# Modulation blocks in the two-stream norms, and four edits beside them, in a float32 network on one core

## The chip, the cores and the metric

The kernel runs on one core of a Trainium2 chip. The metric is the device time of one execution in microseconds (us), lower is better. TensorE is called PE here, VectorE DVE, ScalarE ACT, GpSimd POOL, SyncE SP.

## The reference

The reference is two networks one after the other, all in float32. The first has two layers on two streams, `x` (256 tokens) and `ctx` (256 tokens), width 1024. Each layer computes 9 modulation vectors per stream from `c` and `c_ctx`, and then runs feed-forward, token mixing, feed-forward, each between a norm before and a norm after:

```python
for l in range(DEPTH):                                   # 2
    mx = mod_vectors(c, w_mod[l], b_mod[l])              # silu(c) @ w_mod + b_mod, in 9 parts
    mc = mod_vectors(c_ctx, w_mod[l], b_mod[l])
    x   = sandwich_ffn(x,   gate_up[l, 0], down[l, 0], g[0], g[1], mx[0], mx[1], mx[2])
    ctx = sandwich_ffn(ctx, gate_up[l, 0], down[l, 0], g[0], g[1], mc[0], mc[1], mc[2])
    hx, hc = modulate(rms_norm(x, g[2]), mx[3], mx[4]), modulate(rms_norm(ctx, g[2]), mc[3], mc[4])
    out_x, out_c = token_mix(hx, hc, w_in[l], w_out[l], ...)
    x = x + mx[5] * rms_norm(out_x, g[3])                # ctx the same, but not in the last layer
    x = sandwich_ffn(x, gate_up[l, 1], down[l, 1], g[4], g[5], mx[6], mx[7], mx[8])
```

Token mixing turns queries and keys by rotary factors (cos and sin times the element and its partner 16 rows away), runs attention, and a pooling branch. The second network has four blocks on `x` alone, each with a mixer, a layer norm, an MLP, a layer norm, and a gated projection.

## The kernel before

Every engine walks the same Python program (`walk`) and keeps only its own instructions, so each engine's order is the program order written there. Activations stand as [128 partitions, 8 tiles of channels, tokens]; two-stream stages have n = TT = 512 tokens, one-stream stages n = T = 256.

**Product stages.** Weights come in slots of 1 MB (`w_raw`, four slots, DMA issued by SP, L407). `cut` makes a high part on ACT (`w_hi`, L422) and a low part on DVE (`w_lo`, L425). `slot_products` runs three matmuls per tile pair (L433 to L435): 16 x 3 matmuls for one full slot.

**Modulation.** `w_mod` has 36 blocks of 256 columns per layer, 72 in all. `mod_rows` handles one block: POOL loads two halves of 512 KB into `m_raw` (two buffers, L494), each load waiting until PE has used the same buffer's last content; PE multiplies each half by the two condition vectors (L505), four column groups side by side. After four blocks DVE copies the rows (L512) and `mod_turn` turns them into vectors (L527, L533). The first 8 blocks come from early loads (`m_first`, issued by SP) between the first norm's sums and its tiles. The other 64 are put into product stages, one ahead of a weight slot (`mod_per` in `gemm` and `gate_up`): in layer 0's first feed-forward 16 in gate/up, 8 in the first down product and 4 in the second; in its second feed-forward 16, 8 and 6; in layer 1's first feed-forward 6.

**Norms.** After a product stage `post_norm` waits with `border()` for all engines, takes the root of the sums (`inverse_root`: ACT square root L852, DVE reciprocal L856), and PE broadcasts the result to all partitions with four 128x128 matmuls (`spread`, L781). DVE scales and adds, tile by tile (L944, L949). `pre_norm` of the next stage follows in `pre_sums`: per channel tile k an ACT square (L794) and a PE sum (L774), in lockstep with DVE's tiles by two `tmp_g` buffers; then `inverse_root` again, and DVE and ACT make `a_hi` and `a_lo` (L913, L918, L925), for which the first slot's products wait tile by tile. There are four two-stream pairs of post and pre norm (after both layers' first feed-forward, after layer 0's mixing and second feed-forward).

**repeat_bias.** In both first feed-forwards, just ahead of `post_norm`, POOL issues seven DMAs (L1107) that rewrite a bias table from DRAM to DRAM. POOL reaches them after its last `m_raw` load of the second down product.

**Rotary.** `rope_na` runs between the products of the pooling input: 8 matmuls against a permutation (`na_swap`, L1226), and 24 small DVE operations.

**Layer norms of the second network.** `product_norm` gathers its sums during the products; `centre_of_first` (L1495) sits between the first and second half of pair 1, group 0. Its chain at the end has two broadcasts, `far` and `root`.

Of the kernel before, what the change touches and what calls it, by code (L numbers as in the profile page):

```python
# [29 lines left out]
P = 128  # L30
# [47 lines left out]
class Place:  # L78


    def __init__(self):
        self.slot, self.side, self.tables, self.mod_layer, self.mod_slot = 0, 0, 0, 0, 0
        self.a_ready = None
        self.a_order = None
        self.x_ready = None
# [70 lines left out]
def constants():  # L156
# [5 lines left out]
    swap = np.zeros((P, P), np.float32)  # L162
    for p in range(P):
# [6 lines left out]
        swap[p + (ROPE_PAIRS if first else -ROPE_PAIRS), p] = 1.0  # L170
    c["na_cos"], c["na_sin"], c["na_swap"] = cos, sin, swap
# [44 lines left out]
def build(nc, A, out, upto=99):  # L216

    with ExitStack() as ctx:
# [42 lines left out]
        with ExitStack() as h:  # L261
# [8 lines left out]
            Z["na_swap"] = sb("na_swap_s", [P, P], F32, h)  # L270
# [79 lines left out]
        def walk(who, e):  # L350
# [58 lines left out]
            def cut(m, i=None, step=0, halves=(0, 1)):  # L409
# [3 lines left out]
                for half in halves:  # L413
                    c = slice(half * P, half * P + P)
                    raw, hi, lo = w_raw[:, m % RAW, :, c], cut_slot(w_hi, m)[:, :, c], cut_slot(w_lo, m)[:, :, c]
                    if act:
# [5 lines left out]
                        e.activation(hi, raw, ACT.Copy).then_inc(S.hi_ready.sem, 1)  # L422
                    if dve:
                        e.wait_ge(S.hi_ready.sem, val(2 * m + half + 1, i, 2 * step))
                        e.tensor_tensor(lo, raw, hi.bitcast(F32), ALU.subtract).then_inc(S.lo_ready.sem, 1)  # L425
# [56 lines left out]
            def mod_rows(i, j, per):  # L482


                layer, ms = at.mod_layer, at.mod_slot + j
                w = matrix(A["w_mod"][layer])
# [3 lines left out]
                for half in range(2):  # L490
                    k0 = 4 * half
                    if pool and own >= 1:
                        e.wait_ge(S.mod_used.sem, val(2 * count + half - 1, i, 2 * per))
                        e.dma_start(m_raw[:, half, :, :], w[:, k0:k0 + 4, ms * SC:ms * SC + SC] if i is None  # L494
                                    else w[:, k0:k0 + 4, bass.ds(e.snap(i * (per * SC) + ms * SC), SC)]).then_inc(mod_landed[half], 16)
                    if pe:
                        if half == 0 and r == 0 and batch > 0:
                            e.wait_ge(S.mod_rows.sem, val(batch, i, batches))
                        if own >= 1:
                            e.wait_ge(mod_landed[half], val(16 * own, i, 16 * per))  # L500
                        elif half == 0:
                            e.wait_ge(first_landed[count], 32)
# [43 lines left out]
            def mods(passes, per):  # L546

                def body(i, first):
                    for j in range(per):
                        mod_rows(i, j, per)  # L550
                        if j:
                            mod_turn(i, j - 1, per)
# [1937 lines left out]
```

## Time and profile before

| | us |
|---|---|
| runs (3) | median 3280.05, 3278.34 to 3292.75 |
| profiled execution, own time | 3276.89 |
| its span | 3274.9 |
| PE busy | 3064.8 (94%) |
| DVE busy | 1678.6 (51%) |
| ACT busy | 1354.5 (41%) |
| POOL busy | 213.9 (7%) |

The busy share of PE counts pipelined matmuls as busy and averages over stages. The norms show as stretches in which the granted PE clock falls and PE is idle; the page's slices hide them, the windows show them.

### The profile page before, as it was taken

Reading aid. Unit: us, or ns where it says so; the run is one execution under the profiler, and the core shown is the slowest. Engines: PE = TensorE matmul, PEld = TensorE weight load, DVE = VectorE, ACT = ScalarE, POOL = GpSimd, SP = SyncE. Lnnn points to the kernel's source line nnn. Section 1 sums busy time; section 2 is a strip of 40 time slices with the busy share of each in tenths; the row PEclk is TensorE's granted clock in tenths of the full one; section 3 lists DMA queues with packets and bytes.
Section 4 is the critical chain, followed back from the end, with each engine's and each line's share of the span. In section 5 each row is a group of like instructions: output and inputs, shape, how many; then the busy total and the mean of one; then the engine's idle time right before and its main releaser. Section 6 shows DMA issues by size and latency. Waiting matters only on the chain. (4 is left out here: it accounts for less than half of the span.)

```text
span 3274.9 us, 52918 instructions
## 1 busy us (share of the span) xinstructions
PE 3064.8 (94%) x21712; PEld 2694.9 (82%) x21712; DVE 1678.6 (51%) x2574; ACT 1354.5 (41%) x2092; POOL 213.9 (7%) x304
## 2 busy tenths in 40 slices
PE   6999989989999899997989899998999999988998
PEld 4777858657777688876789889998799989988998
DVE  3332254552322633235655557656675677556765
ACT  3222232632222432223455455546464555454644
POOL 1111014101110000011200000000000000000000
PEclk9999989989999899998989999999899999989999
DMA  8555344135554223253245543554265546543553
GB/s 275 167 179 171 99 133 124 40 104 179 177 167 145 90 90 102 91 163 117 67 146 191 167 154 112 185 168 137 65 193 193 160 146 202 191 141 104 168 193 104
DMA packets 405772, 474.85 MB, mean 145 GB/s; under 512 B 10860, under 2 KB 383164, under 8 KB 405578
## 3 DMA queue, kind: packets, MB, share of 16 engines
q1 hardware_dynamic: 380176, 389.05, 36.9%
q0 software_dynamic: 24544, 82.74, 8.0%
q8 instruction: 144, 2.36, 0.3%
q10 hardware_dynamic: 858, 0.29, 0.0%
q14 instruction: 50, 0.41, 0.0%
HBM read 470.84 MB, written 4.84 MB: 145 GB/s over the span
## 5 line engine op out<-in xcount | busy, mean ns | idle before, releaser
L425 DVE TENSOR_TENSOR w_lo<-w_raw,w_hi 128x1024 fp32r<-128x1024 f32 x734 | 897.3, 1228 | 1268.8 <-ACT w_hi L422 1267.7
L433 PE MATMUL bank<-a_hi,w_hi 128*128 128x256 f32 (+1 forms) x3864 | 1241.3, 321 | 57.8 <-DVE a_lo L1398 16.6
L434 PE MATMUL bank<-a_lo,w_hi 128*128 128x256 f32 (+1 forms) x3864 | 1227.1, 318 | 0.0
L435 PE MATMUL bank<-a_hi,w_lo 128*128 128x256 f32 (+1 forms) x3864 | 1226.3, 317 | 0.0
L422 ACT ACTIVATE w_hi<-w_raw 128x1024 fp32r<-128x1024 f32 x734 | 771.1, 1056 | 987.5 <-PE bank L435 957.1
L433 PEld LDWEIGHTS bank<-a_hi,w_hi 128*128 128x128 f32 x3864 | 741.2, 192 | 134.5 <-issue 76.0
L435 PEld LDWEIGHTS bank<-a_hi,w_lo 128*128 128x128 f32 x3864 | 741.5, 192 | 50.5
L434 PEld LDWEIGHTS bank<-a_lo,w_hi 128*128 128x128 f32 x3864 | 741.4, 192 | 47.7
L433 PE MATMUL bank<-h_hi,w_hi 128*128 128x256 f32 (+1 forms) x1728 | 544.5, 315 | 0.0
L435 PE MATMUL bank<-h_hi,w_lo 128*128 128x256 f32 (+1 forms) x1728 | 539.6, 312 | 0.0
L434 PE MATMUL bank<-h_lo,w_hi 128*128 128x256 f32 (+1 forms) x1728 | 539.5, 312 | 0.0
L433 PEld LDWEIGHTS bank<-h_hi,w_hi 128*128 128x128 f32 x1728 | 325.8, 189 | 29.9 <-issue 7.4
L435 PEld LDWEIGHTS bank<-h_hi,w_lo 128*128 128x128 f32 x1728 | 324.7, 188 | 21.1
L434 PEld LDWEIGHTS bank<-h_lo,w_hi 128*128 128x128 f32 x1728 | 325.0, 188 | 20.0
L494 POOL DMA_DIRECT2D m_raw<-in_w_mod x128 | 95.6, 751 | 1162.7 <-PE bank L505 1017.3
L636 ACT ACTIVATE h_hi<-tmp_y 128x256 f32 (+3 forms) x216 | 94.7, 477 | 84.9 <-DVE tmp_y L689 83.8
L640 DVE TENSOR_TENSOR h_lo<-tmp_y,h_hi 128x256 f32 (+3 forms) x216 | 99.7, 502 | 11.3 <-ACT h_hi L636 9.5
L1682 ACT ACTIVATE tmp_g<-bank 128x256 f32<-128x256 f32 x128 | 49.1, 383 | 128.4 <-PE bank L435 128.4
L774 PE MATMUL bank<-tmp_g,ones 128*32 128x64 f32 (+1 forms) x1040 | 52.8, 292 | 49.7 <-ACT tmp_g L794 46.9
L433 PE MATMUL bank<-w_hi,a_hi 128*128 128x256 f32 (+1 forms) x288 | 82.9, 288 | 10.7 <-DVE v_g L763 10.7
L710 ACT ACTIVATE z<-bank 128x512 f32<-128x512 f32 (+1 forms) x48 | 25.2, 526 | 156.2 <-PE bank L435 156.1
L1107 POOL DMA_DIRECT2D xt<-in_p x4 | 2.9, 732 | 1295.2 <-DVE a_lo L1398 676.9
(289 smaller groups left out, 2320.7 us busy)
## 6 DMA issues: line engine op xcount, KB each, us to landing
w_raw<-in_mlp_w SPq DMA_DIRECT2D x128, 1024.0 KB, 5.3
w_raw<-in_w_ffn_gate_up SPq DMA_DIRECT2D x88, 1024.0 KB, 5.3
m_raw<-in_w_mod POOLq DMA_DIRECT2D x128, 512.0 KB, 4.8
w_raw<-in_w_ffn_down SPq DMA_DIRECT2D x32, 1024.0 KB, 5.9
w_raw<-in_gla_w_in SPq DMA_DIRECT2D x24, 1024.0 KB, 5.5
w_raw<-in_w_in SPq DMA_DIRECT2D x16, 1024.0 KB, 6.0
w_raw<-in_ple_w_gate SPq DMA_DIRECT2D x16, 1024.0 KB, 5.1
w_raw<-in_w_ffn_down SPq DMA_DIRECT2D x16, 768.0 KB, 6.2
```

The source lines that it names most:

```text
L422: e.activation(hi, raw, ACT.Copy).then_inc(S.hi_ready.sem, 1)
L425: e.tensor_tensor(lo, raw, hi.bitcast(F32), ALU.subtract).then_inc(S.lo_ready.sem, 1)
L433: e.matmul(dst, hi, rhs_hi, start=start, stop=False)
L434: e.matmul(dst, hi, rhs_lo, start=False, stop=False)
L435: return e.matmul(dst, lo, rhs_hi, start=False, stop=stop)
L494: e.dma_start(m_raw[:, half, :, :], w[:, k0:k0 + 4, ms * SC:ms * SC + SC] if i is None else w[:, k0:k0 + 4, bass.ds(e.snap(i * (per * SC) ...
L636: e.activation(hidden_at(h_hi_f, p, m, i, per, n), tmp_y[:, m, 0:n], ACT.Copy).then_inc(S.hidden_hi.sem, 1)
L640: e.tensor_tensor(hidden_at(h_lo_f, p, m, i, per, n), tmp_y[:, m, 0:n], hidden_at(h_hi_f, p, m, i, per, n).bitcast(F32), ALU.subtract).the ...
L710: e.activation(dst, b[m][:, 0:n], ACT.Copy).then_inc(S.act_evicted.sem, 1)
L774: mm = e.matmul(dst[32 * g:32 * g + 32, 0:w], ones[:, 0:32], src[:, g * w:g * w + w], start=start, stop=stop)
L1107: e.dma_start(dst, src).then_inc(side_sem, 16)
L1682: e.activation(tmp_g[:, m, 0:T], b[m][:, 0:T], ACT.Relu).then_inc(S.act_evicted.sem, 1)
```

## The change

1. `mod_rows` is split into `mod_load` (POOL), `mod_half` (PE, one half block) and `mod_copy` (DVE). A generator, `mods_in_norm`, puts four blocks into each two-stream post/pre norm pair: both loads of the first block at the top of `post_norm`, its two halves ahead of the root's broadcast, the third half ahead of the next norm's sums, and the other five after sums 1 to 5. The row copy follows the tiles, the turn follows the first slot's products. That makes 16 blocks in norms and 48 in product stages: `ffn` now gets 16 in gate/up and 4 in the second down product for both layers' first feed-forward, and 8 in the first down product for layer 0's second. In a stage that has blocks, the first one now follows the first slot.
2. The broadcast of a root (and of `far`) is done in two halves of 64 rows, into two banks (`spread_halves`).
3. At the start the first blocks run between the first norm's sums, and the first two slots are cut inside its tiles.
4. The rotary partners come from 8 DMAs between partitions (`swap_partners`, POOL); DVE does 6 wide operations instead of 24; the permutation matmuls and PE's wait on `at.roped` are gone.
5. `centre_of_first` moves into the second half's products where a pair has more than one group (the MLPs).

`gate_up` gets the same `opening` lines as `gemm`. `product_norm` calls `spread_halves` for `far` with banks (5, 6) and for `root` with (4, 7).

```diff
@@ -479,37 +477,71 @@
-def mod_rows(i, j, per):
+def mod_load(i, j, per, half):
     layer, ms = at.mod_layer, at.mod_slot + j
...
+    w, count, k0 = matrix(A["w_mod"][layer]), S.mod_used.n // 2 + j, 4 * half
+    if pool and count - FIRST_MODS >= 1:
+        e.wait_ge(S.mod_used.sem, val(2 * count + half - 1, i, 2 * per))
+        e.dma_start(m_raw[:, half, :, :], w[:, k0:k0 + 4, ms * SC:ms * SC + SC] if i is None
+                    else w[:, k0:k0 + 4, bass.ds(e.snap(i * (per * SC) + ms * SC), SC)]).then_inc(mod_landed[half], 16)
+def mod_half(i, j, per, half):
     q, r, size, batches = batch_of(j, per)
...
     own, skip = count - FIRST_MODS, 2 * r
...
+    if pe:
+        if half == 0 and r == 0 and batch > 0:
+            e.wait_ge(S.mod_rows.sem, val(batch, i, batches))
+        if own >= 1:
+            e.wait_ge(mod_landed[half], val(16 * own, i, 16 * per))
+        elif half == 0:
+            e.wait_ge(first_landed[count], 32)
+        src = m_raw[:, half, :, :] if own >= 0 else m_first[:, 2 * count + half, :, :]
+        for g in range(4):
+            mm = e.matmul(b[32 * g:32 * g + 32 - skip, :], c_pad[:, 4 * half + g, skip:], src[:, g, :],
+                          start=r == 0 and half == 0, stop=r == size - 1 and half == 1)
+        mm.then_inc(S.mod_used.sem, 1)
+def mod_copy(i, j, per):
+    q, r, size, batches = batch_of(j, per)
+    b, count, batch = bank[4 + q % 2][:, 0:SC], S.mod_used.n // 2 + j, S.mod_rows.n + q
     if dve and r == size - 1:
...
         e.tensor_copy(at.rows[:, q % 2, :], b).then_inc(S.mod_rows.sem, 1)
+def mod_rows(i, j, per):
+    for half in range(2):
+        mod_load(i, j, per, half)
+        mod_half(i, j, per, half)
+    mod_copy(i, j, per)
+def mods_in_norm():
+    for half in range(2):
+        mod_load(None, 0, MOD_BATCH, half)
+    yield
+    for j in range(MOD_BATCH):
+        for half in range(2):
+            if j:
+                mod_load(None, j, MOD_BATCH, half)
+            mod_half(None, j, MOD_BATCH, half)
+            yield
+    mod_copy(None, MOD_BATCH - 1, MOD_BATCH)
+    yield
+    mod_turn(None, MOD_BATCH - 1, MOD_BATCH)
+    mods_done(MOD_BATCH, 1)
+    yield
+def norm_mods(steps):
+    for _ in range(steps if at.norm_mods else 0):
+        next(at.norm_mods)
@@ -543,16 +575,16 @@
...
+def first_mods(per):
+    for j in range(6):
+        mod_rows(None, j, per)
+        yield
+    mod_turn(None, 3, per)
+    for j in range(6, per):
+        mod_rows(None, j, per)
+    mod_turn(None, per - 1, per)
+    yield
@@ -598,6 +631,11 @@
                                   ready if p == 0 and i is None else None)
+                if opening:
+                    norm_mods(1)
+                    at.norm_mods = None
+                    if mod_per:
+                        mod_rows(i, 0, per * mod_per)
                 if sums and g == 0 and p:
@@ -780,6 +822,21 @@
     mm.then_inc(S.pe.sem, 1)
+def spread_halves(pair, small, n):
+    w = n // 4
+    for g in (0, 2, 1, 3):
+        rows = slice(64 * (g // 2), 64 * (g // 2) + 64)
+        mm = e.matmul(bank[pair[g // 2]][:, (g % 2) * w:(g % 2) * w + w], picks[rows, g, :], small[rows, 0:w],
+                      start=True, stop=True)
+    mm.then_inc(S.pe.sem, 1)
+def halves_of(x):
+    return x.rearrange("p (h t) -> p h t", h=2)
+def in_halves(pair):
+    return banks[:, pair[0]:pair[1] + 1:pair[1] - pair[0], 0:T // 2]
@@ -855,13 +913,14 @@
     S.dve.n += 1
+    norm_mods(beside)
     if pe:
         e.wait_ge(S.dve.sem, S.dve.n)
-        spread(bank[to], small, n)
+        spread_halves(to, small, n)
     S.pe.n += 1
...
         e.wait_ge(S.pe.sem, S.pe.n)
-    at.root = bank[to]
+    at.root = (lambda c: bank[to[c.start // T]][:, 0:T]) if n == TT else (lambda c: in_halves(to))
@@ -882,15 +941,25 @@
-def pre_sums(n, to=7):
-    if at.x_ready:
+def pre_sums(n, to=None, between=None):
+    if between:
+        border()
+        for k in range(DK):
+            column_sum(lambda k: xt[:, k, 0:n], k, DK, n, True)
+            if k % 2:
+                next(between)
+    elif at.x_ready:
         for k in range(DK):
             column_sum(lambda k: xt[:, k, 0:n], k, DK, n, True, (S.dve, at.x_ready[k]))
+            norm_mods(1 if 1 <= k <= 5 else 0)
     else:
...
     at.x_ready = None
+    if between:
+        next(between)
+        next(between)
     inverse_root(n, 1.0, 0, to)
@@ -905,19 +974,26 @@
     lag = len(tiles) // DK + 1
...
     scaled, done = {}, {}
...
             if dve:
...
             S.dve.n += 1
...
             scaled[j] = S.act.n
+        if summed and j == 0:
+            cut(0, lo=False)
+        if summed and j == lag:
+            cut(0, hi=False)
+        if summed and j == len(tiles) - 1:
+            cut(1, lo=False)
         if j >= lag:
@@ -927,22 +1003,30 @@
             done[k] = (S.dve, S.dve.n)
+    if summed:
+        cut(1, hi=False)
+    norm_mods(1)
     at.a_ready = done
+    if n == TT:
+        at.norm_mods = mods_in_norm()
+        norm_mods(1)
     border()
-    inverse_root(n, 1.0, 0)
+    inverse_root(n, 1.0, 0, beside=2)
+    norm_mods(1)
     factor(layer, g_row, chunk, None, times)
...
     base = S.dve.n
...
         if dve and j:
@@ -1214,26 +1298,32 @@
-def rope_na(qk_done):
-    base_p, base_d = S.pe.n, S.dve.n
-    if pe or dve:
-        side_wait()
+def swap_partners(qk_done):
+    if pool:
         e.wait_ge(S.act_evicted.sem, qk_done)
-    for j in range(8):
-        b = bank[4 + j // 2][:, (j % 2) * T:(j % 2) * T + T]
-        if pe:
-            e.matmul(b, Z["na_swap"][:, :], qk[:, j, 0:T], start=True, stop=True).then_inc(S.pe.sem, 1)
+    partner = prob[:].rearrange("p a b t -> p (a b t)").rearrange("p (j t) -> p j t", t=T)
+    for p in range(0, P, 2 * ROPE_PAIRS):
+        low, high = slice(p, p + ROPE_PAIRS), slice(p + ROPE_PAIRS, p + 2 * ROPE_PAIRS)
+        side_load(partner[low, :, :], qk[high, :, 0:T])
+        side_load(partner[high, :, :], qk[low, :, 0:T])
+def rope_na():
+    base = S.dve.n
+    for j in range(2):
+        flat = lambda x: x[:].rearrange("p a b t -> p (a b t)").rearrange("p (j t) -> p j t", t=T)[:, 4 * j:4 * j + 4, :]
+        straight, partner, heads = flat(probT), flat(prob), qk[:, 4 * j:4 * j + 4, 0:T]
+        wide = lambda t: t[:, :].unsqueeze(1).to_broadcast([P, 4, T])
         if dve:
...
+            if j == 0:
+                side_wait()
+            e.tensor_tensor(straight, heads, wide(Z["na_cos"]), ALU.mult).then_inc(S.dve.sem, 1)
+            e.tensor_tensor(partner, partner, wide(Z["na_sin"]), ALU.mult).then_inc(S.dve.sem, 1)
+            e.wait_ge(S.dve.sem, base + 3 * j + 2)
+            e.tensor_tensor(heads, straight, partner, ALU.add).then_inc(S.dve.sem, 1)
+        S.dve.n += 3
+        yield
@@ -1324,9 +1414,9 @@
     gemm(w, [(0, DK)], 2, 2, a_op(TT), copy_to(qk_f[:, 4 * TT:], TT, TT), S.act_evicted, first_col=NA_WIDTH)
-    qk_done = S.act_evicted.n
+    swap_partners(S.act_evicted.n)
     gemm(w, [(0, DK)], 2, 2, a_op(n), copy_to(ut[:].rearrange("p a t -> p (a t)"), TT, n), S.act_evicted,
-         first_col=3 * NA_WIDTH, between=rope_na(qk_done))
+         first_col=3 * NA_WIDTH, between=rope_na())
     pool_windows(n)
@@ -1560,8 +1650,8 @@
             products(n, k0, kt, b, g == 0, end, ready if p == 0 and g == 0 else None,
-                     centre_of_first if p == 1 and g == 0 else None,
-                     {2: totals_early, 3: totals_late}.get(p) if end else None)
+                     centre_of_first if p == 1 and each == 1 else None,
+                     centre_of_first if p == 1 and g == 0 and each > 1 else {2: totals_early, 3: totals_late}.get(p) if end else None)
             if p == 1 and g == 0:
@@ -2410,21 +2500,20 @@
     pad_bias()
-    pre_sums(TT, 6)
-    mods(1, 4)
-    mods(1, 4)
-    at.rows = rows_mod
+    blocks = first_mods(8)
+    pre_sums(TT, (3, 6), blocks)
     if pool or act or dve:
         side_wait()
-    cut(0)
-    cut(1)
+    next(blocks)
+    mods_done(8, 2)
+    at.rows = rows_mod
     yield
...
         last = layer == DEPTH - 1
-        yield ffn(layer, 0, TT, 2 * (not last), 2 * (not last), 2 * last, 1 * (not last))
+        yield ffn(layer, 0, TT, 2, 0, 0, 1)
         yield mix(layer, last)
         if not last:
-            yield ffn(layer, 1, TT, 2, 2, 2)
+            yield ffn(layer, 1, TT, 0, 2, 0)
         else:
```

## Rows read from the trace of the kernel before

**Rows 1.** The page: busy time of the engines.
```profile
PE 3064.8 (94%) x21712; PEld 2694.9 (82%) x21712; DVE 1678.6 (51%) x2574; ACT 1354.5 (41%) x2092; POOL 213.9 (7%) x304
```
**Rows 2.** Windows: stretch, PE, PEld, DVE, ACT, POOL busy, granted clock, DMA share, GB/s.
```profile
450.00:500.00 50.00, 34.48 (x193) 25.29 (x194) 31.66 (x73) 19.25 (x35) 8.25 (x14) 0.73 0.28 83
```
**Rows 3.** Timeline of PE (start, duration, instruction): round a block in gate/up (112.92, left out).
```profile
112.61 0.39 PE L435 MATMUL bank<-a_hi,w_lo 128*128 128x512 f32 x1
...
113.92 0.50 PE L433 MATMUL bank<-a_hi,w_hi 128*128 128x512 f32 x1
114.26 0.39 PE L434 MATMUL bank<-a_lo,w_hi 128*128 128x512 f32 x1
```
**Rows 4.** Timeline: the first block of layer 0's second feed-forward.
```profile
693.96 1.94 PE L505 MATMUL bank<-m_raw,c_pad 128*32 128x256 f32 x16
...
697.22 0.47 PE L433 MATMUL bank<-a_hi,w_hi 128*128 128x512 f32 x1 [1.32 <-issue]
```
**Rows 5.** Timeline: layer 0's first post norm and the next pre norm.
```profile
451.38 0.37 SPq L407 DMA_DIRECT2D w_raw<-in_w_in  x1
451.80 0.37 ACT L852 ACTIVATE r_tmp<-bank,stat 128x128 f32<-128x128 f32 x1 [0.67 <-PE bank L774]
...
453.40 1.88 PE L781 MATMUL bank<-r_tmp,picks 128*128 128x128 f32 x8 [1.79 <-DVE r_tmp L856]
...
458.18 0.65 PE L774 MATMUL bank<-tmp_g,ones 128*32 128x128 f32 x8 [2.90 <-ACT tmp_g L794]
...
468.02 0.65 PE L774 MATMUL bank<-tmp_g,ones 128*32 128x128 f32 x8 [0.41 <-ACT tmp_g L794]
...
475.57 0.76 PE L433 MATMUL bank<-a_hi,w_hi 128*128 128x512 f32 x1 [3.34 <-DVE a_lo L925]
```
**Rows 6.** Window of 2 us after that norm; columns as in rows 2.
```profile
480.00:482.00 2.00, 2.00 (x8) 1.61 (x7) 2.00 (x7) 1.21 (x3) 0.00 (x0) 0.78 0.00 0
```
**Rows 7.** Timeline of POOL ahead of layer 0's first post norm.
```profile
430.87 1.49 POOL L494 DMA_DIRECT2D m_raw<-in_w_mod  x2 [8.12 <-PE bank L505]
...
444.27 2.38 POOL L1107 DMA_DIRECT2D rpb_rows<-rpb_pad  x3 [8.26 <-issue]
452.58 0.79 POOL L1107 DMA_DIRECT2D rpb_rows<-rpb_pad  x1 [5.93 <-issue]
```
**Rows 8.** DMA issues at 452.6, 674.2, 710.3: KB, us to landing.
```profile
rpb_rows<-rpb_pad POOLq DMA_DIRECT2D x1, 254.0 KB, 5.4
...
m_raw<-in_w_mod POOLq DMA_DIRECT2D x1, 512.0 KB, 6.6
...
m_raw<-in_w_mod POOLq DMA_DIRECT2D x1, 512.0 KB, 3.9
```
**Rows 9.** Timeline of PE: the permutation matmuls of layer 0.
```profile
532.60 3.62 PE L1226 MATMUL bank<-qk,na_swap_s 128*128 128x256 f32 x16
535.87 0.58 PE L433 MATMUL bank<-a_hi,w_hi 128*128 128x512 f32 x1
```
**Rows 10.** The start: the early loads (page's form), then the timeline.
```profile
m_first<-in_w_mod SPq DMA_DIRECT2D x14, 512.0 KB, 9.3
...
39.34 2.01 ACT L422 ACTIVATE w_hi<-w_raw 128x1024 fp32r<-128x1024 f32 x2 [10.08 <-DMA w_raw<-in_w_ffn_gate_up]
...
42.82 4.62 DVE L425 TENSOR_TENSOR w_lo<-w_raw,w_hi 128x1024 fp32r<-128x1024 f32 x4
...
47.56 1.66 DVE L913 SCALAR_TENSOR_TENSOR z<-xt,fac,bank 128x256 f32<-128x256 f32 x4
```
**Rows 11.** Timeline: attention scores of two 64-row pairs.
```profile
570.10 1.99 PE L1009 MATMUL bank<-qk 64*128 64x512 f32 x8
```
**Rows 12.** Chain that ended last: the broadcast of a layer norm's root.
```profile
3053.36 1.12 PE bank L781 x8
```
**Rows 13.** Timeline of PE: the centre's sum in an MLP's product.
```profile
2133.85 0.59 PE L1495 MATMUL bank<-tmp_y,ones 128*128 128x256 f32 x2
2134.09 0.47 PE L433 MATMUL bank<-h_hi,w_hi 128*128 128x256 f32 x1
```

More of the change, by code:

```diff
@@ L407, in load, with cut @@
                 e.dma_start(dst, s).then_inc(landed[n % RAW], 16)
-            def cut(m, i=None, step=0, halves=(0, 1)):
+            def cut(m, i=None, step=0, halves=(0, 1), hi=True, lo=True):
                 if total and m >= total[0]:
@@ L489, in mod_rows @@
                 own, skip = count - FIRST_MODS, 2 * r
[L490 to L495, printed above, removed]
-                    if pe:
[L497 to L502, printed above, removed]
-                        src = m_raw[:, half, :, :] if own >= 0 else m_first[:, 2 * count + half, :, :]
-                        for g in range(4):
-                            mm = e.matmul(b[32 * g:32 * g + 32 - skip, :], c_pad[:, k0 + g, skip:], src[:, g, :],
-                                          start=r == 0 and half == 0, stop=r == size - 1 and half == 1)
-                        mm.then_inc(S.mod_used.sem, 1)
+                if pe:
[13 more added lines that the diff above has]
+                b, count, batch = bank[4 + q % 2][:, 0:SC], S.mod_used.n // 2 + j, S.mod_rows.n + q
                 if dve and r == size - 1:
@@ L544, in mods_done @@
                     at.mod_layer, at.mod_slot = at.mod_layer + 1, 0
[L546 to L552, printed above, removed]
-                    mod_turn(i, per - 1, per)
-                rep(passes, body, loads=True)
-                mods_done(passes * per, passes * batch_of(0, per)[3])
+            def first_mods(per):
[7 more added lines that the diff above has]
+                yield
             def mod_vec(layer, chunk):
@@ L587, in body @@
                         for g, (k0, kt) in enumerate(kgs):
-                            if mod_per:
+                            opening = i is None and p == 0 and g == 0
+                            if mod_per and not opening:
                                 mod_rows(i, p * mod_per + g, per * mod_per)
@@ L662, in body @@
                             s += 1
-                            if mod_per:
+                            opening = i is None and p == 0 and half == 0
+                            if mod_per and not opening:
                                 mod_rows(i, 2 * p + half, 2 * per)
@@ L1635, in product_norm @@
                     e.wait_ge(S.dve.sem, S.dve.n)
-                    spread(root, small, T)
+                    spread_halves(root, small, T)
                 S.pe.n += 1
```

59 lines of the change are left out of this document (26 added, 33 removed).

## The prediction, made blind

> **What bounds the kernel now.** I read the page's busy times first, then windows of 50 us over the whole span, then timelines of the stretches that stood out, then the DMA answers. PE is busy 94% of the span [rows 1]; in the product stages matmul follows matmul at the full clock, 0.39 us each when started 0.227 apart [rows 3]. There an instruction taken off PE is time taken off the span. The exceptions are the norms: in the window of layer 0's first one PE is busy 34 of 50 us and the granted clock's mean is 0.73 [rows 2]. Inside a norm the path runs over DVE: from the square root at 451.80 to the first product at 475.57 are 23.8 us, in which PE does two broadcasts and eight sums [rows 5]. There PE's idle time is free, but an instruction at which PE waits, ahead of a broadcast or a sum, is on the path. The change takes work from the first kind of place to the second. What it gains is sure; what it pays depends on where PE stands when a load lands.
>
> **Blocks out of the product stages.** In a stage the matmuls start every 0.227 us. Round a block, 113.92 - 112.61 = 1.31 us pass, of which 0.23 is the usual step, and the next matmul comes 0.11 late (the following start was 114.26): 1.2 us a block [rows 3]. Sixteen blocks leave. One was free already: the first block of layer 0's second feed-forward ran from 693.96 to 695.90, and the first product came only at 697.22, since it waits for DVE [rows 4]. 15 x 1.2 = 18.0 us gained. It also did a service: broadcast and block kept PE at work without a break, the clock was at its upper level at 697.22 (matmul 0.47 us, against 0.76 us at 475.57 in the norm without a block, [rows 4, 5]). There some 12 matmuls ran 0.43 us apart until the window 480 to 482, whose mean granted clock is 0.78, between the two levels of 1.2 and 2.4 GHz [rows 6]: 12 x (0.43 - 0.23) = 2.4 us, which this stage will now pay. That is -2.4.
>
> **Blocks in the norms: the loads.** Two buffers, each reloaded only after use. A half's load alone takes 3.9 us from issue to landing, beside a 1 MB weight load 6.6 us [rows 8]. A block is 1.31 - 0.23 = 1.08 us at the full clock and took 1.94 across the change of clock [rows 3, 4], so a half is 0.54 to 1.08 us. SP issues one weight load at the start of each of these norms (451.38, [rows 5]).
>
> Norms without bias DMAs (layer 0's mixing and second feed-forward). The first two halves have long landed and run beside the square root and the reciprocal, done by 452.7, ahead of the broadcast at 453.40: free. The third half's load is issued at about 452.3 and meets the weight load: lands at 458.9, runs to 460.0, where the first sum stood at 458.18 [rows 5]. From there each buffer turns round in 3.9 + 1.08 + 0.2 for the two semaphores = 5.2 us, against 2 x 1.45 us for two of the old sums (458.18 to 468.02 are 9.8 us for seven steps, the last shorter). Following both buffers and the sums in PE's order: halves end at 460.0, 462.4, 465.2, 467.5, 470.4, 472.7, the last sums at 474.0 instead of 468.7: 5.3 us late, or about 4 with the clock up. I take 5.0, x 2 = 10.0 us lost. Bounds: 0 (loads so quick that the sums' slack covers them) and 8.
>
> Norms behind `repeat_bias` (both layers' first feed-forward). Here POOL's order decides. The last bias DMA is issued at 452.58, 0.8 us after the square root has begun [rows 5, 7]; the norm's first two loads stand behind it, and PE's first two halves stand ahead of the broadcast. The bias DMA needs 5.4 us to land [rows 8], so until 458.0; the first load follows it in POOL's queue, landing at about 459.2, the second at 460.5 (1 MB beside a load costs it 6.6 - 3.9 = 2.7 us, so 512 KB move in about 1.3). Halves end 460.3 and 461.6, the broadcast at 462.8 instead of 455.3: 7.5 us late. The rest goes as above and adds 4.3: 11.8, or 9.8 with the clock up, since two halves, a broadcast and a half are nearly as long a run as the one at 692 to 696 after which the clock was up. I take 11.0, x 2 = 22.0 us lost. Layer 1 gets the same four blocks ahead of its bias DMAs as layer 0, whose last block load stands 21.7 us before the last bias issue [rows 7], so its issues fall alike. Bounds: 5 (bias issues earlier) and 25 (below). Everything queued on PE behind a half waits, and DVE waits for the broadcast.
>
> **The rule on the shared engines.** The trace has 3.9 against 6.6 us for the same load, alone and beside weights [rows 8]. "Trainium Kernel Development and Optimization", Key Constraints, in the Trainium skill says that DMAs from SP, ACT and POOL run on the same 16 engines and interleave; by it the weight load at the norm's start slows the third half, and a separate issuing queue is no cover. The trace agrees.
>
> **Broadcasts in halves.** A two-stream broadcast takes 1.88 to 2.08 us, a one-stream one 1.12 [rows 5, 12]. Sixteen full-height float32 records of 256 columns took 3.62 us, 0.23 each [rows 9], so 512 columns should take 0.45; eight 64-row records of 512 columns took 1.99 us, 0.25 each [rows 11], so pairs in different row halves run beside each other. I take 0.6 of the old time: 0.85 and 0.45 us gained. The four two-stream broadcasts of pre norms count (those of post norms are in the sums above): 3.4; three one-stream norms 1.35; eight roots of layer norms 3.6 (`far` lies beside the square root). 8.4 us. Bounds: 0 (no overlap) and 10. "TensorE: Matmul & The Clock Gate", Part 3, in the Trainium skill has a packing of four row tiles at 3.07 times; by its kind of gain two would come near the half, an estimate that would put the broadcasts at 9.6 rather than 8.4.
>
> **Rotary.** 535.87 - 532.60 = 3.27 us [rows 9], plus 0.18 for a next matmul that is late as the one behind a block is: 3.45, twice: 6.9 us gained. The 8 DMAs go out when the keys are evicted, a slot ahead of the pooling input's second slot; at 0.79 us an issue [rows 7] and some 3 us to land (below the 3.9 of a load with three to four times their bytes, [rows 8]) they are there after about 9 us. In layer 0 a slot lasts 48 x 0.227 = 11 us, so nothing waits; in layer 1 it lasts 5.4 and DVE waits some 4 us, but its next cut is wanted only after a whole slot of 11 us. If that cover fails, 4 us are lost. Bounds 3 and 6.9.
>
> **The centre's sum.** In the MLPs it never waited: the product behind it starts 0.24 us later, with no idle time listed ahead of it [rows 13]. Moving it gains nothing, -0.2 to 0.3.
>
> **The start.** The early loads are issued every 1.7 us and land after 9.3 [rows 10], block j at about 12 + 3.4 j us: 0 to 5 can run among the sums and beside the root, 6 and 7 at 32 to 38 us. The factors are there at about 39.8 instead of 47.4, and the first weight slot at 39.3 [rows 10]. So the tiles begin 7.7 us earlier than at 47.56, but half of the 4.62 us of low cuts now lies among them: 7.7 - 2.3 = 5.4, and 5.5 us gained is my value. Bounds: 2 (blocks delayed by their loads, the square root's table load behind them) and 7.7.
>
> **The sum.** Gains 18.0 + 8.4 + 6.9 + 5.5 = 38.8; losses 2.4 + 10.0 + 22.0 = 34.4. Net -4.4 us on the profiled execution's 3276.89, so 3272.5. The median of the runs is 3.2 us above the profiled one; carried over, 3275.7. I give 3275.
>
> **The rivals.**
> *Covered waits.* The loads land inside the slack: 0 for the plain norms and 5 for the bias ones, so 38.8 - 2.4 - 10 = 26 us gained, 3254. For it: late in the norm the DMA engines move nothing (0.00 of their time, [rows 6]). Against it: turning a buffer round takes 5.2 us and POOL's order is fixed. In the same direction, a clock kept up into the first slot would give 2.4 us in each of four norms, 3265; against it is that PE has 6.9 us between the last sum and the first product with one broadcast in it [rows 5], and the clock was at half after the same gap.
> *POOL's issues stall (the other side).* Behind groups of bias DMAs POOL stood 8.26 and 5.93 us with no releaser in the trace [rows 7]. If that is room in its queue, and the norm's loads behind the last bias DMA meet it twice in eight, each bias norm loses 2 x 5.9 = 11.8 more: +23.6, 3299, slower. It decides from 20 us of stall in all. For it: the pauses came in every group of bias DMAs. Against: the pause of the block loads in the same rows, 8.12, has PE's block as its releaser, and after the pause of 5.93 only one bias DMA is outstanding.
> *Broadcasts do not overlap and the start gains little:* 8.4 and 3 back: 3287.
>
> **How the numbers follow.** The forecast, with its own range of 3263 to 3285, 0.48; covered waits or clock up 0.29; stall 0.11; no overlap or a small mixture above 0.12. One half of a per cent, 16 us, is about what a measurement of this kernel can tell from no change: below 3263.6 faster, above 3296.4 slower. Faster holds nearly all of the second case and a little of the first: 0.31. Slower is the stall with a little of the last: 0.12. Same: 0.57. Range 3248 to 3292: it leaves out the stall and the far end of the covered case.
>
> **What would show it.** In the changed trace: in the two bias norms the broadcast (L781's heir) starts some 7 us later after the square root than 1.6 us, with PE idle ahead of a half block until the DMA of `m_raw`; in the plain ones only sums are late. PE's idle time ahead of half blocks should come to 20 to 35 us in all. No blocks in layer 0's second gate/up, period of a block 12.1 us elsewhere. The first product at about 46 us. Broadcasts at 1.2 and 0.65 us. It is wrong if PE's wait for `m_raw` comes to under 10 us, if the first halves in the bias norms have landed before the square root, or if POOL shows pauses between loads inside a norm.

## The result, and the profile after

The changed kernel takes 3318.67 us in the median of four runs (3309.43 to 3330.73), the kernel before 3280.53 beside it: ratio 1.0104, 95% interval 1.0071 to 1.0136. By the ratio it is slower by about 34 us; the forecast was 3275, the range ended at 3292, and a slower kernel had been given a chance of 0.12. The profiled execution took 3316.82 us, its span 3315.1 against 3274.9.

The page, busy time of the engines, to be read beside [rows 1]:

```profile
PE 3055.7 (92%) x21676; PEld 2686.0 (81%) x21676; DVE 1678.4 (51%) x2536; ACT 1353.7 (41%) x2092; POOL 229.4 (7%) x318
```

PE does 9 us less and the span is 40 us longer, so PE waits some 49 us more. The waits of PE that a block load ended, in all, times, longest (after, then before):

```profile
PE bank L503 <- DMA m_raw<-in_w_mod: 80.1, 34, 10.2
```
```profile
PE bank L505 <- DMA m_raw<-in_w_mod: 7.2, 2, 6.4
```

The forecast had 20 to 35 us here. Of the 80.1, 55.4 stand in the four norms and 24.2 in five other places, to which the text comes below. The timeline of PE in layer 0's first norm, which answers to [rows 5]:

```profile
450.37 0.94 PE L816 MATMUL bank<-tmp_g,ones 128*32 128x128 f32 x16 [0.77 <-ACT tmp_g L851]
460.47 2.30 PE L503 MATMUL bank<-m_raw,c_pad 128*32 128x256 f32 x16 [9.16 <-DMA m_raw<-in_w_mod]
462.70 1.23 PE L831 MATMUL bank<-r_tmp,picks 64*128 64x128 f32 x8
466.20 1.08 PE L503 MATMUL bank<-m_raw,c_pad 128*30 128x256 f32 x8 [2.27 <-DMA m_raw<-in_w_mod]
...
476.92 1.07 PE L503 MATMUL bank<-m_raw,c_pad 128*26 128x256 f32 x8 [1.32 <-DMA m_raw<-in_w_mod]
477.76 0.66 PE L816 MATMUL bank<-tmp_g,ones 128*32 128x128 f32 x8
479.76 1.07 PE L503 MATMUL bank<-m_raw,c_pad 128*26 128x256 f32 x8 [1.35 <-DMA m_raw<-in_w_mod]
480.61 1.08 PE L816 MATMUL bank<-tmp_g,ones 128*32 128x128 f32 x16
483.17 1.23 PE L831 MATMUL bank<-r_tmp,picks 64*128 64x128 f32 x8 [1.48 <-DVE r_tmp L914]
487.75 0.77 PE L431 MATMUL bank<-a_hi,w_hi 128*128 128x512 f32 x1 [3.36 <-DVE a_lo L1001]
```

The first halves hold the broadcast back for 9 us, and most of the later sums stand behind a half that waits for its load. The timeline of POOL there, answering to [rows 7], says why: the last bias DMA goes out at 451.44, the first two loads right behind it, and every later load when PE has used the buffer.

```profile
443.70 2.37 POOL L1191 DMA_DIRECT2D rpb_rows<-rpb_pad  x3 [7.03 <-issue]
451.44 0.80 POOL L1191 DMA_DIRECT2D rpb_rows<-rpb_pad  x1 [5.37 <-issue]
452.24 1.58 POOL L486 DMA_DIRECT2D m_raw<-in_w_mod  x2
462.16 0.75 POOL L486 DMA_DIRECT2D m_raw<-in_w_mod  x1 [8.35 <-PE bank L503]
```

That much was forecast. What was not stands between the first and the second slot of the first product stage:

```profile
58.03 0.39 PE L433 MATMUL bank<-a_hi,w_lo 128*128 128x512 f32 x1
58.35 1.07 PE L503 MATMUL bank<-m_raw,c_pad 128*32 128x256 f32 x16
63.77 1.01 PE L503 MATMUL bank<-m_raw,c_pad 128*30 128x256 f32 x8 [4.35 <-DMA m_raw<-in_w_mod]
65.50 1.08 PE L503 MATMUL bank<-m_raw,c_pad 128*30 128x256 f32 x8 [0.72 <-DMA m_raw<-in_w_mod]
66.51 0.79 PE L431 MATMUL bank<-a_hi,w_hi 128*128 128x512 f32 x1
67.10 0.63 PE L432 MATMUL bank<-a_lo,w_hi 128*128 128x512 f32 x1
...
70.52 0.49 PE L431 MATMUL bank<-a_hi,w_hi 128*128 128x512 f32 x1
70.84 0.39 PE L432 MATMUL bank<-a_lo,w_hi 128*128 128x512 f32 x1
```

The first block of the stage, moved behind the first slot, is next to the second. The second's loads can go out only when the first has used the buffers (POOL, below), so PE stands 4.35 + 0.72 us inside a product stage. Behind the pause ten products start 0.43 us apart, not 0.23: another 10 x 0.2 = 2 us. Five stages open like this (at 58, 412, 896, 1134 and 1488 us); the first of each pair of waits is 4.35, 4.01, 3.94, 3.84 and 3.96 us, and 10, 6, 8, 7 and 12 products behind them start 0.43 us apart. Over all five the waits come to 24.2 us and the slow products to 8.9.

```profile
59.32 1.49 POOL L486 DMA_DIRECT2D m_raw<-in_w_mod  x2 [20.42 <-PE bank L503]
65.09 0.75 POOL L486 DMA_DIRECT2D m_raw<-in_w_mod  x1 [4.28 <-PE bank L503]
```

To see where time goes I cut every span at the start of ACT's square root in each norm (L852 before, L910 after). All numbers are us between two such rows, each from the one profiled execution of its version. "Norm" is from a post norm's root to the pre norm's; "part" is the stage between them, from a pre norm's root to the next post norm's. FF is a feed-forward.

| | before | after | e1 | e2 | e3 | e6 | e10 |
|---|---|---|---|---|---|---|---|
| part: layer 0, first FF | 422.9 | 420.7 | 408.7 | 421.7 | 418.5 | 408.1 | 406.9 |
| norm (bias DMAs) | 16.9 | 30.3 | 30.2 | 22.0 | 15.8 | 21.8 | 15.5 |
| part: layer 0, mixing | 204.9 | 198.9 | 199.4 | 200.5 | 200.1 | 200.2 | 199.1 |
| norm | 16.9 | 22.2 | 21.8 | 22.1 | 15.8 | 22.0 | 15.5 |
| part: layer 0, second FF | 410.1 | 389.6 | 383.4 | 391.2 | 410.2 | 383.2 | 382.9 |
| norm | 17.1 | 22.4 | 22.1 | 22.6 | 15.8 | 23.0 | 15.5 |
| part: layer 1, first FF | 381.4 | 413.9 | 397.6 | 413.8 | 380.6 | 397.2 | 395.8 |
| norm (bias DMAs) | 16.4 | 31.7 | 30.9 | 21.6 | 15.8 | 22.0 | 15.5 |
| part: layer 1, mixing | 142.5 | 143.6 | 142.8 | 143.0 | 145.2 | 143.1 | 142.6 |
| from the last root to the end | 1415.1 | 1411.5 | 1406.4 | 1407.5 | 1411.8 | 1425.1 | 1408.1 |

Between layer 1's mixing and the last root stand one norm (9.0 to 10.3) and one feed-forward (189.7 to 191.4 in the versions shown). The last row scatters from 1404 to 1425 between executions, although its instructions are the same in every version but the kernel before and e5 (1415.1 and 1413.8, the second network as it was). Edits in the first network are therefore judged by its stages, and whole kernels by ratios of medians.

### The profile page after: what moved, and what is told of

The parts are those of the page before. It is cut to its first block and busy times, and to the rows that moved or that the text cites. A ratio compares the mean times of both kernels' runs of the same rounds, so it can differ in the third digit from the quotient of the medians.

```text
span 3315.1 us, 52811 instructions
## 1 busy us (share of the span) xinstructions
PE 3055.7 (92%) x21676; PEld 2686.0 (81%) x21676; DVE 1678.4 (51%) x2536; ACT 1353.7 (41%) x2092; POOL 229.4 (7%) x318
## 5 line engine op out<-in xcount | busy, mean ns | idle before, releaser
L503 PE MATMUL bank<-m_raw,c_pad 128*26 128x256 f32 (+3 forms) x1040 | 89.0, 452 | 80.7 <-DMA m_raw<-in_w_mod 80.1
L503 PEld LDWEIGHTS bank<-m_raw,c_pad 128*26 128x26 f32 (+3 forms) x1040 | 27.3, 115 | 117.6 <-DMA m_raw<-in_w_mod 77.5
```

The source lines that it names most:

```text
L503: mm = e.matmul(b[32 * g:32 * g + 32 - skip, :], c_pad[:, 4 * half + g, skip:], src[:, g, :], start=r == 0 and half == 0, stop=r == size - ...
```

## The experiments

**e1: the turn inside the norm, no shifted opening.** The theory: the loss that the forecast lacks is the openings.

```diff
 def mods_in_norm():          # the end of it
+    at.odd = 1               # the row buffer that the next batch does not use
     mod_copy(None, MOD_BATCH - 1, MOD_BATCH)
-    yield
     mod_turn(None, MOD_BATCH - 1, MOD_BATCH)
     mods_done(MOD_BATCH, 1)
+    at.odd = 0
 # gemm and gate_up
-                if mod_per and not opening:
+                if mod_per:
                     mod_rows(...)
-                if opening: norm_mods(1); ...; mod_rows(i, 0, ...)
```

> The changed kernel, with the turn of the norm's eight pieces back inside the norm (copy by ACT and turn by PE behind the last sum, in the second row buffer), so that every slot has its block ahead of it again, the first slot too. Theory of the openings: in the changed kernel five stages open with two blocks next to each other, the second waits 3.8 to 4.4 us for its load, and some 8 to 20 us of products run at or near the half clock behind it, 6 to 8 us in each: 5 x 6.5 = 32 us come back, less about 1 us in each of four norms for the copy and the turn, so 3318 goes to about 3290, and PE's wait for the block loads falls from 80 us by about 20. Rival, the norms' own blocks: these cost all of the loss, the stages behind them run slowly because PE has stood in the norm, and the order of blocks at the opening is without effect: 3318 to 3322. Rival, a small one: only the wait for the load comes back, 5 x 4 us, 3302.

(The copy stayed on DVE in the kernel that ran; only its place and its row buffer changed.)

Measured: 3285.37 us, ratio to before 1.0017 (0.9998 to 1.0036), against 1.0104 for the changed kernel. The parts with two openings give 12.0 and 16.3 us, the part with one 6.2: 34.5 us, 6.9 each. The norms stay as they were or get a little shorter, so copy and turn cost nothing there. PE's waits for block loads are 61.8 us, 18.3 less: the 24.2 us at the openings are gone, the norms have 2.1 less, and 8.5 stand ahead of the very first product (0.5 in the changed kernel), where a block now comes before it again. With the 8.9 us of slow products the openings account for 33.1 us, close to the 34.5; how the price of that first block and the halves' own time at the lower clock offset each other was not measured.

**e5: the shifted opening alone, in the kernel before.**

```diff
+                opening = i is None and p == 0 and g == 0
-                if mod_per:
+                if mod_per and not opening:
                     mod_rows(i, p * mod_per + g, per * mod_per)
 ...                                     # the slot's products
+                if opening and mod_per:
+                    mod_rows(i, 0, per * mod_per)
```

> The kernel before with one thing of the change alone: the first block of a stage stands behind the first slot's products instead of ahead of them, next to the second block; no block is in a norm and none of the four small edits is made. Putting the turn back in the norm gave 12.0 us over two such openings, 6.2 over one and 16.3 over two, 6.9 each. Theory of the openings: the same price in this kernel, for up to seven openings, +30 to +50 us: 3280 goes to 3310 to 3330. Rival, the price comes only with the blocks in the norms (rows waiting to be turned, a clock that fell in the norm): within 5 us of before.

Measured: 3339.99 us, ratio 1.0173 (1.0151 to 1.0195). The seven openings cost 21.8 us (three, 422.9 to 444.7), 25.7 (three, 410.1 to 435.8) and 7.0 (one, 381.4 to 388.4): 7.8 each. With +58 us the whole lies above the 30 to 50 that were expected. The first of them in PE's timeline is the picture of the changed kernel:

```profile
66.30 1.07 PE L505 MATMUL bank<-m_raw,c_pad 128*32 128x256 f32 x16
71.47 1.08 PE L505 MATMUL bank<-m_raw,c_pad 128*30 128x256 f32 x8 [4.10 <-DMA m_raw<-in_w_mod]
73.14 1.08 PE L505 MATMUL bank<-m_raw,c_pad 128*30 128x256 f32 x8 [0.59 <-DMA m_raw<-in_w_mod]
74.15 0.80 PE L433 MATMUL bank<-a_hi,w_hi 128*128 128x512 f32 x1
```

No block is in a norm here, so the price is the order's own: put in alone it costs 7.8 us an opening, and taken out (e1) it gives back 6.9.

**e2: the bias DMAs ahead of the second gate/up part.**

```diff
     for j, (t0, tiles) in enumerate(parts):
+        if f == 0 and j == 1:
+            repeat_bias(layer)
         gate_up(...)
 ...
-    if f == 0:
-        repeat_bias(layer)
     post_norm(...)
```

> The changed kernel, with the bias DMAs issued on POOL ahead of the second gate/up part instead of ahead of the norm. Theory of POOL's order: the two bias norms, 30.3 and 31.7 us from root to root, become like the plain ones, 22.2 and 22.4, and 8 + 10 = 18 us come back: 3300. Rival, the bias DMAs cost the same wherever they stand: they hold up block loads inside the products, one or two blocks wait some 5 us each in both layers, and 0 to 8 us come back: 3311 to 3318.

Measured: 3306.49 us, ratio 1.0076 (1.0053 to 1.0100). The bias norms are like the plain ones, 22.0 and 21.6, 18.3 us less; the parts ahead of them are within about 1 us of what they were (421.7, 413.8). POOL's order was the whole difference between the two kinds of norm. The whole times show less of it, 0.28% or 9 us between the two ratios, with intervals that overlap. In PE's timeline the first halves run beside the root (at 452.60), and the broadcast starts 1.5 us after it; in the changed kernel it was 11.2 us:

```profile
452.64 1.07 PE L503 MATMUL bank<-m_raw,c_pad 128*32 128x256 f32 x16 [0.23 <-issue]
454.11 0.72 PE L831 MATMUL bank<-r_tmp,picks 64*128 64x128 f32 x8 [0.40 <-DVE r_tmp L914]
459.16 1.08 PE L503 MATMUL bank<-m_raw,c_pad 128*30 128x256 f32 x8 [4.34 <-DMA m_raw<-in_w_mod]
```

**e6: e1 and e2 together.**

> Both: the turn back inside the norm, and the bias DMAs ahead of the second gate/up part. Theory: the two are in different places and add, 3318 - 28 - 18 = 3272; with the four small edits worth some 16 of that, sixteen blocks in the norms would then be worth -8 to +8 us. Rival of the norms' own cost: 3300 or more.

Measured: 3273.04 us, ratio 0.9962 (0.9945 to 0.9979). The two causes add up, stage by stage: the parts are as in e1 (408.1, 383.2, 397.2) and the bias norms as in e2 (21.8, 22.0).

**e3: the four small edits alone.** The norm's blocks are taken out and `ffn` gets the block counts of before.

```diff
-    if n == TT:
-        at.norm_mods = mods_in_norm()
-        norm_mods(1)
-        yield ffn(layer, 0, TT, 2, 0, 0, 1)
+        yield ffn(layer, 0, TT, 2 * (not last), 2 * (not last), 2 * last, 1 * (not last))
-            yield ffn(layer, 1, TT, 0, 2, 0)
+            yield ffn(layer, 1, TT, 2, 2, 2)
```

> The kernel before with the four small edits alone (broadcasts in row halves, partners by DMA, the centre's sum a product later, the start's blocks among the sums); no blocks in the norms, blocks ahead of every slot as before. By the stages of the changed kernel: start 7.3 us, broadcasts 8.4 and rotary 3.5 gained, rotary in layer 1 about 3 lost again: 3280 goes to about 3264. Rival, the four edits carry part of the loss (DVE and POOL working beside each other in layer 1's mixing, an opening that costs what it gains): 3275 to 3285.

Measured: 3259.32 us, ratio 0.9931 (0.9904 to 0.9958), 22.6 us less than before. Against e6 it shows the trade itself: in e6 the feed-forward parts are shorter by 10.4 and 27.0 us and longer by 16.6, together 20.8 for 16 blocks, 1.3 each; its four norms are longer by 6.1, 6.2, 7.2 and 6.3, together 25.7. Even mended, the blocks in the norms lost 5 us on balance.

**e4: no reloads in the norm.** Six of a norm's eight half blocks multiply what is already in the buffers, so later modulation is not the reference's.

```diff
     for j in range(MOD_BATCH):
         for half in range(2):
-            if j:
-                mod_load(None, j, MOD_BATCH, half)
             mod_half(None, j, MOD_BATCH, half)
```

> The changed kernel with six of the eight half-block loads of each norm left out (those halves multiply old data, so the modulation of later layers is not the reference's). Theory of the turn-round: PE waits in the norm for loads, so the plain norms go from 22.3 us to about 19 (PE work of six halves of 1.08 less what the sums' idle time takes in), the bias ones, whose first two loads remain behind the bias DMAs, from 31 to 25 or 26. Rival, PE's own time at the half clock is the price: 22 and 30 stay. Between them stands how much of the 39 us that the norms lost is waiting: by the theory some 17.

Measured: one execution, 3303.27 us, so only its stages are read. The plain norms are 15.9 and 15.5 us, what they are with no block at all in e3 (15.8); the bias norms 25.6 and 26.5. The halves fit between the sums without moving them:

```profile
684.80 0.66 PE L817 MATMUL bank<-tmp_g,ones 128*32 128x128 f32 x8
685.23 1.08 PE L504 MATMUL bank<-m_raw,c_pad 128*28 128x256 f32 x8
686.25 0.65 PE L817 MATMUL bank<-tmp_g,ones 128*32 128x128 f32 x8
686.68 1.08 PE L504 MATMUL bank<-m_raw,c_pad 128*28 128x256 f32 x8
687.71 0.66 PE L817 MATMUL bank<-tmp_g,ones 128*32 128x128 f32 x8
```

Sums stand 1.45 us apart with halves of 1.08 between them. PE's work in a plain norm is free; the waiting for loads is all that it costs, 6.3 and 6.9 us and not the 3 that I expected.

**e7 and e9: the rotary partners.** e7 is e3 with the permutation matmuls of before in both layers; e9 has the DMAs in layer 0 and the matmuls in layer 1.

```diff
-    swap_partners(S.act_evicted.n)
+    if not last:
+        swap_partners(qk_done)
-    gemm(..., between=rope_na())
+    gemm(..., between=rope_na_pe(qk_done) if last else rope_na())
```

> The four small edits without the one for the rotary partners: PE's eight permutation matmuls as before. In the four-edit kernel layer 0's mixing (root of the norm before it to root of the one behind) was 4.8 us shorter than in the kernel before, layer 1's 2.7 us longer. Theory: in layer 0 the DMAs give 3.4 us, in layer 1 they land after 16 us and cost about 4 to 5; without them layer 0 goes from 200.1 to 203.5 and layer 1 from 145.2 to 141 or 142; in all the time stays at 3259 plus or minus 3. Rival, layer 1 is longer for another reason (broadcasts, the order of cuts): 145 stays, 3263.

> The four small edits, with the rotary partners by DMA in layer 0, where a slot lasts 11 us, and by PE's permutation in layer 1, where it lasts 5.4. Theory: layer 0's mixing 200 us and layer 1's 141 or 142: 3 to 4 us less than the four edits, 3255. Rival, the layer is not what matters: 3259 as the four edits.

Measured: e7 3263.53 us, ratio 0.9941 (0.9920 to 0.9961); e9 3256.61, 0.9926 (0.9908 to 0.9945). Layer 0's mixing is 202.4 us in e7 against 200.1 (e3) and 199.5 (e9); layer 1's 141.7 and 141.6 against 145.2. So in these kernels the DMAs give 2 to 3 us in layer 0 and cost 3.5 in layer 1. By whole times alone the three can't be told apart. In e3 POOL paused among the partner DMAs themselves:

```profile
1561.26 1.05 POOL L1178 DMA_DIRECT2D prob<-qk  x2 [10.57 <-issue]
```

In the changed kernel, e1, e6 and e10 it did not, and with the same DMAs their layer 1 takes 142.6 to 143.6 us, 1 to 2 above e7 and e9. The wait is there too. The changed kernel's layer 1, DVE first, then POOL:

```profile
1621.68 1.23 DVE L1321 TENSOR_TENSOR probT<-qk,na_cos_s 128x1024 f32<-128x1024 f32 x1 [8.34 <-DMA prob<-qk]
```
```profile
1602.31 2.73 POOL L1191 DMA_DIRECT2D bias<-rpb_rows  x4 [5.95 <-issue]
1605.89 4.21 POOL L1191 DMA_DIRECT2D prob<-qk  x8 [0.85 <-ACT qk L766]
1621.71 0.37 POOL L1357 MEMSET pool_a<- 128x320 f32 x1 [11.60 <-DMA prob<-qk]
```

Eight issues take 4.2 us, and the last lands 16 us after the first issue; POOL's pooling windows stand behind them too. In the same stretch stand 1 MB weight loads and the bias tables issued just before (issues between 1590 and 1611: KB each, median us to landing):

```profile
w_raw<-in_w_out SPq DMA_DIRECT2D x2, 1024.0 KB, 9.9
bias<-rpb_rows POOLq DMA_DIRECT2D x11, 128.0 KB, 4.1
prob<-qk POOLq DMA_DIRECT2D x8, 128.0 KB, 6.5
```

**e10 and e11: six more buffers.** e4 says what a norm needs: the loads there, not fewer of them. The hidden tile is read by nothing from a stage's last product to the next stage's first eviction, and has room for six half blocks (24 KB a partition). e10 is e6 with the third to eighth half loaded there at the norm's start; e11 has the rotary partners of e9 as well.

```diff
+    m_norm = sb("m_norm", [P, 6, 4, SC], F32, h)      # over h_hi
+def norm_load(j, half):
+    ms, k0 = at.mod_slot + j, 4 * half
+    if pool:
+        if j == 1 and half == 0:
+            e.wait_ge(S.slot_used.sem, 2 * at.slot)
+        e.dma_start(m_norm[:, 2 * j + half - 2, :, :], matrix(A["w_mod"][at.mod_layer])[...]
+                    ).then_inc(norm_landed[2 * j + half - 2], 16)
 def mods_in_norm():
     for half in range(2):
         mod_load(None, 0, MOD_BATCH, half)
+    for j in range(1, MOD_BATCH):
+        for half in range(2):
+            norm_load(j, half)
     yield
```

> The kernel with the turn in the norm and the bias DMAs early, and with six more half-block buffers (24 KB a partition, in the hidden tile, which nothing reads between the last product of a stage and the first eviction of the next): six of a norm's eight half blocks are loaded into them at the norm's start, none waits for a buffer to be used. With six loads left out, the plain norms were 15.7 us, as long as without any block (15.8). Theory of the turn-round: the four norms, 22 us each, go to 16 or 17, -21: 3273 goes to 3252, 7 below the four small edits alone. Rival, six loads of 512 KB at once beside the 1 MB weight load take as long as the turn-round did (1.3 us each, the last one landed 8 to 10 us after the first issue) and the norms stay at 20 or more: 3265 to 3273.

> The same, with the rotary partners by DMA in layer 0 alone. Theory: another 3 us, 3249, the lowest of all. Rival as above: 3262 to 3270, above the four edits with the partners by layer (3257).

Measured: e10 3238.02 us, ratio 0.9874 (0.9849 to 0.9898); e11 3236.09, 0.9874 (0.9850 to 0.9899). Both are about 41 us below the kernel before and some 75 below the changed one. All four norms are 15.5 us, 0.3 shorter than with no block in them (15.8 in e3), and below the 16 or 17 that I expected. The six loads go out in 4.45 us at the stage's end, and no half waits for one (timeline of all engines, cut to POOL's loads and PE):

```profile
434.73 4.45 POOL L500 DMA_DIRECT2D m_norm<-in_w_mod  x6 [7.30 <-PE bank L438]
...
437.28 1.07 PE L519 MATMUL bank<-m_raw,c_pad 128*32 128x256 f32 x16 [0.23 <-issue]
...
438.75 0.72 PE L841 MATMUL bank<-r_tmp,picks 64*128 64x128 f32 x8 [0.40 <-DVE r_tmp L924]
...
439.39 0.64 PE L519 MATMUL bank<-m_norm,c_pad 128*30 128x256 f32 x8
...
448.25 0.65 PE L826 MATMUL bank<-tmp_g,ones 128*32 128x128 f32 x8
...
448.68 0.79 PE L519 MATMUL bank<-m_norm,c_pad 128*26 128x256 f32 x8
...
449.70 0.43 PE L826 MATMUL bank<-tmp_g,ones 128*32 128x128 f32 x8 [0.24 <-ACT tmp_g L861]
```

The rotary edit by layer did not give its 3 us: e11's layer 1 mixing took 151.8 us against 142.6 in e10 and 141.6 in e9, since both DVE and PE wait there for the attention's bias tables before they may turn anything:

```profile
1533.13 6.19 PE L1354 MATMUL bank<-qk,na_swap_s 128*128 128x256 f32 x16 [6.43 <-DMA bias<-rpb_rows]
```
```profile
1510.80 4.75 POOL L1208 DMA_DIRECT2D bias<-rpb_rows  x7 [9.30 <-issue]
1523.40 2.72 POOL L1208 DMA_DIRECT2D bias<-rpb_rows  x4 [7.85 <-issue]
```

POOL begins with the tables of this stage no later than in e9 (32.3 us behind the norm's root, 32.9 in e9). Its two pauses are longer, 17.2 us for 12.2, and the last group goes out 61.8 us behind the root, not 55.9. The wait is 6.4 of the 10 us between e11 and e9; the rest was not followed up.

## Why the prediction was wrong

**The step that failed** is the one that has no term. The forecast took the blocks that leave the product stages at 1.2 us each and those that stay at nothing new, although the change says that in a stage with blocks "the first one now follows the first slot". The prediction's own loads show the price: a buffer takes 3.9 us to load [rows 8], and it charged that turn-round to every half in a norm and never to the two blocks that the new order puts side by side. Five openings cost 34.5 us (e1), 6.9 each; 7.8 each in e5. From the forecast's -4.4 to the measured +40.2 on the profiled executions are 44.6 us: these are 34.5 of them, the norms below 7.1, and the other 3 are small things of both signs.

**Blocks out of the product stages**, 18.0 us: right in kind and a little small, 20.8 for the sixteen (e6 against e3). **The cold first slot** of layer 0's second feed-forward: the mark is there (first product 0.77 us at 708.78, where it was 0.47 in [rows 4]), and nine products start 0.43 us apart, 1.8 us in all where 2.4 were forecast. The reason given for it is incomplete. In e3 the block stands ahead of that slot as before, and ten products run slowly all the same: from 680 us to 688 the granted clock stays at 0.50, its lower level, where the kernel before has a mean of 0.58 up to the first product and 1.00 from there. Of e3's edits only the broadcast in halves (1.23 us for 2.08) stands at this place, so it is the likely cause; its own term leaves this loss out.

**The norms.** Plain ones +5.0 each: measured +5.3 and +5.3. Behind the bias DMAs +11.0 each: +13.3 and +15.3 (30.26 - 16.94, 31.68 - 16.43). The mechanism is the one forecast: the first loads behind the last bias DMA, then turn-round by turn-round. The size was 7 us small in all. The first half starts 9.0 us behind the root in layer 0 and 10.0 in layer 1, where the forecast had 7.4: the last bias DMA took 7.5 and 7.7 us to land, not 5.4, and in layer 1 it went out 0.9 us later against the root, though the issues were said to fall alike. The clock stayed at its lower level too (all but one of the halves behind the broadcasts 1.08 us), where I had counted on some of it being up. e2 confirms POOL's order, e4 the turn-round. The 0.2 us for two semaphores in the turn-round has no row behind it.

**The four small edits**, 20.8 us: in sum right, 22.6 in e3, between 14 and 31 by its interval. Its parts differ, so it is partly luck that the sum came out. Broadcasts: 1.23 us where one took 1.88 [rows 5], as forecast; of the eight roots of layer norms five take 0.66 us, as forecast, and three 1.12, no less than before (1.10). A norm without blocks is 1.1 us shorter (15.8, before 16.9). The Trainium skill, "TensorE: Matmul & The Clock Gate", Part 3, has row tiles running beside each other. Here two row halves took 1.23 us for 1.88, 1.5 times as fast and not twice. (The old times that the term goes by, 20.8 us in all, give 10.4 at exactly the half, above its 9.6 and its bound of 10.) The start: e3's first product is at 47.57 us, before 51.97: 4.4, not 5.5, and its next ten products run slowly, where five did; at the next root, 448.40 for 451.80, 3.4 us are left. Rotary: 6.9 forecast, about -1 measured (e3 against e7). Taking the matmuls out gave 2.3 to 2.9 us in layer 0, not 3.45. In layer 1 the wait of some 4 us that a slot was to cover was 8.3 in the changed kernel, since the DMAs landed after 16 us and not 9, and the cover failed. (The 0.18 in the term is 0.11 at the block that it is taken from, [rows 3].) The centre's sum was not tested alone; the scatter of the second network would hide it.

**The rivals.** Covered waits: wrong with two buffers (every norm waits), right with eight (e10). A clock kept up into the first slot: no, the first product after the norm took 0.77 us. POOL's issues stall: no, the norm's two loads went out in 1.58 us right behind the bias DMA, in layer 1 in 1.59, and the pauses between later loads have PE's block as their releaser, but for 0.2 us in each. No overlap of the broadcasts: no. The result lies above all of them, since none had the opening in it; the chance of 0.12 for slower was put mostly on the stall, which did not happen.

## What to carry to other kernels

When an order changes, price the neighbours of what is moved, not the moved piece: two users of a double buffer that come to stand side by side pay a whole load, here 4 to 5 us of waiting and then 1 to 2.5 us of slow products, inside a stage that never waited. Work put into another engine's shadow is free only if its data are there at the shadow's start: with two buffers the sixteen blocks lost 5 us on balance; with eight they gained 25 by the same stages (e10 against e3), 19 by the whole times. Cut the span at one instruction that every version has, and a loss spread over many stages is found in one table.

## What the runs showed of the hardware that was not expected

After a pause of 4 to 5.5 us in the middle of a product stage, the next 6 to 12 products start at half speed (0.43 us apart for 0.23): in the changed kernel 8.9 us behind 24.2 us of waiting, over a third again. The eight halves of a norm with their data there did not lengthen it, and in e10's first norm the clock was back at its upper level before the last sums (0.43 us a sum at 449.70, 0.65 before). POOL paused between groups of DMA issues with no releaser in the trace in every version: 7.03 and 5.37 us in the changed kernel, 10.57 in e3 among the rotary partners, 9.30 and 7.85 in e11 ahead of the bias tables that layer 1 then waited for; what it waits for there stays open. And the stretch from the last root to the end took 1403.8 us in one profiled execution (e11) and 1425.1 in another (e6) with the same instructions. The traces show where. PE's wait for the load of `g_carry` is 5.4 us in e6 and 0.5 in e11, and some product stages run a few per cent slower throughout: 427 products in 50 us, where the same stage has 444 in e11, at a granted clock of 1.00 in both (columns as in [rows 2], e6 first):

```profile
2399.48:2449.48 50.00, 50.00 (x427) 50.00 (x426) 34.59 (x55) 29.46 (x54) 0.00 (x0) 1.00 0.59 186
```
```profile
2378.49:2428.49 50.00, 50.00 (x444) 50.00 (x443) 34.19 (x53) 28.72 (x53) 0.00 (x0) 1.00 0.59 197
```

Why they do stays open.
